# Five small reorderings at the seams of a two-block transformer kernel on one core

## The reference

```
def stick_breaking_attention(q, k, v):          # block 1, 8 heads of 64
    z = einsum('bhqd,bhkd->bhqk', qb, kb) * scale
    log_keep = where(mask, log_sigmoid(-z), 0.0)             # -softplus(z)
    suffix = cumsum(log_keep, reverse=True) - log_keep
    weights = where(mask, exp(log_sigmoid(z) + suffix), 0.0)
    ...
rv = proj columns for the values of retention   # block 1, "ret_v"
...
s = where(valid, (q_lat . c_sel + q_rope . r_sel) * scale, -inf)   # block 2, 8 sparse heads
p = softmax(s, axis=-1)                         # and 8 dilated heads after them
...
sc = einsum('bshd,bmhd->bhsm', qc, kvc[:, :, 0]) * CROSS_HEAD_DIM ** -0.5   # 4 heads of 256
pc = softmax(sc, axis=-1)
oc = einsum('bhsm,bmhd->bshd', pc, kvc[:, :, 1])
x = x + oc @ w_o_cross
x = x + square(relu(rmsnorm(x, norm_mlp_g) @ w_up)) @ w_down
return rmsnorm(x, norm_final_g)
```

## Time and profile before

| what | value |
|---|---|
| time, median of 3 runs (lowest, highest) | 1667.63 us (1666.0, 1667.67) |
| the profiled execution: time, span | 1664.19 us, 1662.4 us |
| PE busy | 1621.7 us, 98% of the span |
| weight loads of PE | 1318.5 us, 79% |
| DVE, ACT, POOL busy | 924.4 us (56%), 733.0 us (44%), 605.3 us (36%) |
| one split of a chunk on POOL (L148, mean of 91), on ACT (L142) | 4.61 us, 1.91 us |
| mean granted TensorE clock | 0.995 of full speed |

### The profile page before, as it was taken

One profiled execution on the slowest core, in us unless ns is written; L12 is line 12 of the kernel. 1 busy time (PEld: TensorE's weight loads), 2 busy tenths in 40 slices (PEclk: granted clock), 3 DMA queues, 4 the chain that ended last, 5 costly groups with the idle time before them and its releaser, 6 DMA issues.

```text
span 1662.4 us, 21089 instructions
## 1 busy us (share of the span) xinstructions
PE 1621.7 (98%) x7972; PEld 1318.5 (79%) x7972; DVE 924.4 (56%) x1116; ACT 733.0 (44%) x880; POOL 605.3 (36%) x253
## 2 busy tenths in 40 slices
PE   9999999999999999999999999999999999999996
PEld 7988888588887888888898668667877888888885
DVE  6244210682465799898967689893433552232313
ACT  5345222334344788878853332674333322221221
POOL 1412264134342243222313645663422444344441
PEclk9999999999999999999999999999999999999998
DMA  5211153212235999999954314101321222222221
GB/s 195 102 52 51 38 152 114 79 73 101 101 107 178 396 421 406 390 392 395 376 228 146 101 63 154 67 1 48 132 74 51 79 98 101 101 101 89 95 95 51
DMA packets 47139, 249.25 MB, mean 150 GB/s; under 512 B 9472, under 2 KB 10240, under 8 KB 20704
## 3 DMA queue, kind: packets, MB, share of 16 engines
q1 hardware_dynamic: 40880, 235.75, 38.2%
q0 software_dynamic: 5184, 8.40, 1.3%
q10 hardware_dynamic: 1008, 4.19, 0.6%
HBM read 236.05 MB, written 16.78 MB: 152 GB/s over the span
## 4 chain that ended last, share of the span: by engine, by line
PE 77%; issue 11%; DVE 6%; POOL 3%; ACT 2%; DMA 1%; SPq 0%; POOLq 0%; DVEq 0%; ACTq 0%
PE psum L229 22%; PE psum L231 21%; PE psum L230 21%; POOL w_lo L148 3%; PE psum L2208 2%; DVE kept_bias L2075 1%; DVE top L2074 1%; PE psum L662 1%; PE psum L2243 1%; PE psum L2231 1%; PE psum L1244 1%; PE psum L2479 1%; PE psum L681 1%; DMA raw<-in_w_dense 1%; PE psum L2499 1%
## 5 line engine op out<-in xcount | busy, mean ns | idle before, releaser
L148 POOL TENSOR_TENSOR w_lo<-raw,w_hi 128x2048 fp32r<-128x2048 f32 x91 | 419.2, 4606 | 701.6 <-ACT w_hi L142 663.3
L142 ACT ACTIVATE w_hi<-raw 128x2048 fp32r<-128x2048 f32 x96 | 183.4, 1910 | 313.8 <-PE psum L231 313.8
L229 PE MATMUL psum<-x_hi,w_hi 128*128 128x512 f32 x808 | 316.5, 392 | 1.4 <-POOL w_lo L148 0.7
L230 PE MATMUL psum<-x_lo,w_hi 128*128 128x512 f32 x808 | 314.4, 389 | 0.0
L231 PE MATMUL psum<-x_hi,w_lo 128*128 128x512 f32 x808 | 314.4, 389 | 0.0
L1262 DVE TENSOR_TENSOR moe_lo<-moe_w,moe_hi 128x2048 fp32r<-128x2048 f32 x100 | 227.7, 2290 | 31.0 <-ACT moe_hi L1252 29.9
L1252 ACT ACTIVATE moe_hi<-moe_w 128x2048 fp32r<-128x2048 f32 x100 | 190.9, 1915 | 30.1 <-PE psum L231 17.8
L229 PEld LDWEIGHTS psum<-x_hi,w_hi 128*128 128x128 f32 x808 | 151.7, 188 | 35.0 <-issue 2.0
L230 PEld LDWEIGHTS psum<-x_lo,w_hi 128*128 128x128 f32 x808 | 151.7, 188 | 31.7 <-issue 0.7
L231 PEld LDWEIGHTS psum<-x_hi,w_lo 128*128 128x128 f32 x808 | 151.7, 188 | 31.7
L434 DVE TENSOR_TENSOR res<-res,psum 128x512 f32<-128x512 f32 x56 | 38.4, 687 | 214.4 <-PE psum L231 214.4
(11 more groups left out here) (377 smaller groups left out, 2914.7 us busy)
## 6 DMA issues: line engine op xcount, KB each, us to landing
raw<-in_w_dense SPq DMA_DIRECT2D x96, 1024.0 KB, 4.8
moe_w<-in_w_moe_ahead SPq DMA_DIRECT2D x54, 1024.0 KB, 14.3
moe_w<-in_w_moe SPq DMA_DIRECT2D x48, 1024.0 KB
yrow<-expert_rows SPq DMA_DIRECT2D x8, 512.0 KB, 7.9
res<-in_x SPq DMA_DIRECT2D x4, 512.0 KB, 6.4
decay<-in_decay SPq DMA_DIRECT2D x8, 256.0 KB, 5.0
hn_rows<-hn_tok ACTq DMA_DIRECT2D x4, 512.0 KB, 7.8
out<-res SPq DMA_DIRECT2D x4, 512.0 KB, 2.7
```

The lines of the kernel that those rows point to most:

```text
L142: act.activation(w_hi[c % RING][:, :], raw[c % RING][:, :], ACT.Copy).then_inc(hi_ready, 1)
L148: pool.tensor_tensor(w_lo[c % RING][:, :], raw[c % RING][:, :], w_hi[c % RING][:, :].bitcast(F32), ALU.subtract).then_inc(lo_ready, 1)
L229: pe.matmul(out, lh, rh, start=first, stop=False)
L230: pe.matmul(out, lh, rl, start=False, stop=False)
```

## The change

Nothing that is computed changes. What moves:

1. In stick-breaking DVE makes `softplus(0)` before `size(1)` and `logs_low(0)` before it reads out tile 2.
2. The second tile of a head that has two (tiles 4, 6, 8, 10 and 13: `SECOND_V`) goes to bank 6 and not to bank 7. Bank 6 also holds the values of a pair of heads, so such a tile waits for `y_low` of the pair before from head 2 on, and `values` waits until bank 6 is read out.
3. ACT loads the exp table behind the sixth tile of v_b, takes the first exp of head 0 (`weigh(act, 0, 0)`) behind the seventh, and splits the second chunk of out2 (`split_hi`) only behind the exps of head 1. POOL's `split_lo` of that chunk moves behind all of its normalising in attention. DVE normalises head 0 before the softmax of head 1. dil_bias is loaded ahead of the chunks that v_b loads.
4. In cross attention the last head is turned into banks 4 and 5, which are spent once exp(2) is done, so that `transposes(2)` and `transposes(3)` stand before `values(2)` and `values(3)`. On DVE `normalise(3)` stands before the roundings of head 1.
5. The last norm sums squares by token: matmuls with one output column give 128x4 sums, root and reciprocal are taken of 128x4, DVE widens the result to 128x512 (`last_wide`), four transposes spread it in bank 5, and the eight scalings read it from PSUM. The square of the last tile is not added by DVE; it is a second group of four matmuls into the same columns.

```
@@ sticks_tensor, sticks_vector
+    SECOND_V = [tiles_of(h)[1] for h in range(HEADS) if TILES_V[h] == 2]
-            if j >= 1:
-                pe.wait_ge(bank_free, V_T + j + 4)
+            if j in SECOND_V:
+                pe.wait_ge(bank_free, V_T + j + 3)
+            elif j >= 1:
+                pe.wait_ge(bank_free, V_T + j + 4 - (j - 1 in SECOND_V))
...
+            pe.wait_ge(bank_free, V_T + 4 + max(j + 1 for j in SECOND_V if j < UPTO_V[min(2 * p + 1, HEADS - 1)]))
...
+                if j in SECOND_V and h >= 2:
+                    pe.wait_ge(y_low, h // 2)
                 ret_v_tile(j)
...
+        softplus(0)
         size(1)
-        softplus(0)
+        logs_low(0)
         ret_v_out(2)
-        logs_low(0)
@@ project_sync, project_gpsimd, project_scalar
+                if name == "v_b":
+                    sp.wait_ge(x1_done, KT)
+                    sp.wait_ge(tables_done, 4)
+                    sp.wait_ge(bank_free, FIRST_TILE["q_rope"] + 4)
+                    sp.dma_start(dil_bias[:, :], d["dil_bias"]).then_inc(a_in, 16)
...
-        dense_pool(pool, "v_b")
+        dense_pool(pool, "v_b", splits=1)
...
-            scale=tok_r12[:, j % 4:j % 4 + 1]).then_inc(bank_free, 1))
+            scale=tok_r12[:, j % 4:j % 4 + 1]).then_inc(bank_free, 1), splits=1,
+            tile_hooks={5: lambda: act.preload_act_table_set("exp_and_others"), 6: lambda: weigh(act, 0, 0)})
@@ attend_vector, attend_scalar, attend_gpsimd
+        softmax(0, 0)
+        softmax(0, 1)
         normalise(0)
+        softmax(1, 0)
+        softmax(1, 1)
...
-        exp(1, 0)
-        exp(1, 1)
+        weigh(act, 1, 0)
+        weigh(act, 1, 1)
+        split_hi(act, FIRST_CHUNK["out2"] + 1, FIRST_TILE["out2"])
...
             ins.then_inc(s_norm_pool, 1)
+        split_lo(pool, FIRST_CHUNK["out2"] + 1)
@@ cross_stage_tensor
-            if h >= 1:
+            if h == CH_HEADS - 1:
+                pe.wait_ge(cs_exp, COUNTED + CH_HEADS - 1)
+            elif h >= 1:
                 pe.wait_ge(ct_read2, COUNTED + h)
...
-        for h in range(CH_HEADS):
+        for h in range(CH_HEADS - 2):
             transposes(h)
-            if h + 2 < CH_HEADS:
-                scores(h + 2)
+            scores(h + 2)
+            values(h)
+        for h in range(CH_HEADS - 2, CH_HEADS):
+            transposes(h)
+        for h in range(CH_HEADS - 2, CH_HEADS):
             values(h)
@@ mlp_vector
+        dve.wait_ge(last_rooted, ONCE + 1)
+        link(dve, dve.reciprocal(last_rstd[:, :], last_rms[:, :]))
+        dve.tensor_copy(last_wide[:, :, :], wide(last_rstd[:, :], [P, TB, P], 2)).then_inc(last_turned, 1)
+        dve.wait_ge(last_spread, ONCE + 1)
+        for kt in range(KT):
...
+            dve.scalar_tensor_tensor(out=res[:, kt, :], in0=res[:, kt, :], scalar=norm_end2.gain_of(kt),
+                                     in1=psum[:, 5, :], op0=ALU.mult, op1=ALU.mult).then_inc(n_scaled, 1)
@@ mlp_tensor
-        norm_end2.pe(pe)
+        pe.wait_ge(n_added, (KT - 1) * norm_end2.u + KT - 2)
+        for q in range(TB):
+            pe.matmul(psum[:, 4, q:q + 1], norm_end2.sum[:, q * P:(q + 1) * P], ones[:, 0:1], start=(q == 0), stop=False,
+                      skip_group_check=True)
+        pe.wait_ge(n_squared, KT * (norm_end2.u + 1))
+        for q in range(TB):
+            mm = pe.matmul(psum[:, 4, q:q + 1], norm_end2.sq[1][:, q * P:(q + 1) * P], ones[:, 0:1], start=False, stop=True,
+                           skip_group_check=True)
+        mm.then_inc(last_summed, 1)
+        pe.wait_ge(last_turned, ONCE + 1)
+        for q in range(TB):
+            mm = pe.transpose(psum[:, 5, q * P:(q + 1) * P], last_wide[:, q, :], ident[:, :])
+        mm.then_inc(last_spread, 1)
```

More of the change, by code:

```diff
@@ L176, in dense_sync, with dense_pool @@
         loop(sp, n, body)
-    def dense_pool(pool, name, after=None, halves_first=False):
+    def dense_pool(pool, name, after=None, halves_first=False, splits=2):
         n, k = turns(name)
@@ L189, in dense_pool, with dense_act @@
         loop(pool, n, body)
-    def dense_act(act, name, evac=None, hooks=None, ahead=True):
+    def dense_act(act, name, evac=None, hooks=None, ahead=True, tile_hooks=None, splits=2):
         n, k = turns(name)
@@ L204, in body @@
                     evac(act, i, j, (t0 + j) % 4)
-                if ahead or i < n - 1:
+                    if tile_hooks and j in tile_hooks:
+                        tile_hooks[j]()
+                if b < splits and (ahead or i < n - 1):
                     split_hi(act, c0 + 2 + b, t0 + per * (b + 1), i, k * per * i)
@@ L2313, in attend_vector, with weigh @@
                 low((k - 3) // 2)
+    def weigh(act, h, part):
+        b = h % 3
+        scale = (HD + 32) ** -0.5 if h < HEADS else HD ** -0.5
+        act.wait_ge(s_read, COUNTED + 2 * h + part + 1)
+        for qt in ((3,), (2, 1, 0))[part]:
+            n = P * (qt + 1)
+            ins = act.activation(score_of(h)[:, SEG[n]:SEG[n] + n], score_of(h)[:, SEG[n]:SEG[n] + n], ACT.Exp,
+                                 bias=snmax[b][:, qt:qt + 1], scale=scale, accum_out=ssum[b][:, qt:qt + 1])
+        if part:
+            ins.then_inc(s_exp, 1)
     def attend_scalar(act):
@@ L2350, in attend_scalar @@
             if k + 2 < A_HEADS:
-                exp(k + 2, 0)
+                weigh(act, k + 2, 0)
             if k < A_HEADS:
@@ L2415, in high @@
             act.activation(y_hi[:, t, :], psum[:, 2 + t % 2, :], ACT.Copy).then_inc(cv_high, 1)
-        for h in range(CH_HEADS):
+        for h in range(CH_HEADS - 2):
             copy_t(h)
-            if h + 2 < CH_HEADS:
-                exp(h + 2)
+            exp(h + 2)
             high(2 * h)
             high(2 * h + 1)
+        for h in range(CH_HEADS - 2, CH_HEADS):
+            copy_t(h)
+        for t in range(2 * CH_HEADS - 4, 2 * CH_HEADS):
+            high(t)
         residual_act(act, "o_cross", norm_mlp, root=False, gained=lambda t: norm_mlp.high_gained(act, t))
@@ L2551, in mlp_scalar @@
             else:
-                residual_act(act, name, norm_end2)
+                residual_act(act, name, norm_end2, root=False)
+                act.wait_ge(last_summed, ONCE + 1)
+                act.activation(last_rms[:, :], psum[:, 4, 0:TB], ACT.Sqrt, scale=1.0 / D, bias=col("eps"))\
+                   .then_inc(last_rooted, 1)
     def mlp_vector(dve):
@@ L2604, in _ @@
             project_sync(sp)
-            attend_sync(sp)
             cross_stage_sync(sp)
```

58 lines of the change are left out of this document (29 added, 29 removed).

## The result

The changed kernel takes 1654.72 us (median of 5 runs, 1654.38 to 1660.36) against 1667.63 before: ratio 0.993, 95% interval 0.9916 to 0.9944. It is faster by 0.7%, or 11.7 us by the ratio and 12.9 by the medians. The forecast of 1656.9 was 2.2 us high; its gain of 10.7 us is less than either figure.

What follows compares the result with a forecast made beforehand. TensorE, busy 98% of the span, was taken to bound the kernel. Terms of -1.45, -3.75, 0, 0, -1.9 and -3.6 sum to -10.7 us, giving 1656.9 from the median 1667.63; range 1653.5 to 1661.5.

Steps and rivals of the forecast that it cites:

- first hole of stick-breaking: TensorE's 1.4 us wait before the first suffix sums goes as softplus(0) starts earlier on DVE: -1.45 us.
- bank 6, five places: Stick-breaking: five second value tiles no longer wait for the first one's copy, 0.75 us each: -3.75 us.
- attention's start: The wait at head 0 goes, but the same time is waited at heads 1 and 2: 0, bounds -2.2 and +0.9.
- POOL's split, dil_bias: Split after attention ends 8.6 us before out2 wants the chunk; dil_bias loads on an almost empty queue: cost 0.
- cross attention: Values of heads 2 and 3 run without a hole, one of about 0.7 stays: -1.9 us, bounds -2.3 and -1.0.
- tail: Last norm: 3.1 us from a shorter chain, square to first scaling, 0.5 from shorter scalings: -3.6, bounds -4.0 and -2.5.
- the holes only move: Rival in stick-breaking: bank 7's holes only move, the stage gives 1.4 instead of 5.2 us, total 1660.7; 8%.
- attention gains too: Rival at attention's start: ACT's split is hidden and both holes go, sum -12.9 us, total 1654.7; 12%.
- the half microsecond for a shorter step of the scalings: Tail: eight scalings with an operand in PSUM step in 0.60 instead of 0.67 us, 0.5 us gained.
- Slower by GpSimd: Rival at out2's second chunk: each microsecond POOL's split ends after 1141.9 is one of TensorE; 1671 us, 3%.
- the turning point: Delay of POOL's split from which the kernel is slower than before by 3.3 us: 22.6 us (8.6 + 10.7 + 3.3).

Runs made afterwards that it cites:

- the one run with a delay: The changed kernel with GpSimd's moved split of out2's second chunk done four times over, each waiting for the one before: 1664.10 us in one run.
- the second measurement: The same changed kernel run once more with nothing altered: 1654.39 us, ratio 0.9929 to the kernel before.

## Why the prediction was right

Each step of the forecast against what the traces give:

| step | forecast | measured |
|---|---|---|
| first hole of stick-breaking | -1.45 | -1.80 |
| bank 6, five places | -3.75 | -3.98 |
| attention's start | 0 (-2.2 to 0.9) | -0.16 |
| POOL's split, dil_bias | 0, cover 8.6 | 0, cover 8.7 |
| cross attention | -1.9 | -1.99 |
| tail | -3.6 | -3.26 |
| sum | -10.7 | -11.2 |

- **Stick-breaking.** Order and waits are as forecast, none of the new waits (`y_low`, bank 6) shows. Both terms were too small, by 0.35 and by 0.23, because the way back to pace was priced at 0.05 for the one hole and 0.19 for each of the others; it was 0.4 and 0.24. The rival that the holes only move is refuted by each edit run alone.
- **Attention.** The two holes that take the first one's place are where the forecast said, at head 1 and at the scores of head 4, and the price of the split decides between them and a gain: with it moved, 0.62 came. The rival "attention gains too" overrated its prize: with the split hidden the stage gave 0.8 in all and not 2.2, as DVE is next.
- **Cross attention.** One hole of 0.65 in front of transposes(3), forecast 0.7; the values of both heads without a gap. The roundings that values(3) wants, forecast 0.1 us ahead of need, end 0.20 ahead of its matmuls.
- **Tail.** The chain was right: 2.82 for 2.95 from the last square to the first scaling; the widening took 0.43, less than its estimate of 0.55. The mis-sized term is the half microsecond for a shorter step of the scalings. It was read off scalings that multiply by a number, and went to scalings that multiply by a column; the 0.06 us a step are the column's. The Trainium skill (VectorE: DVE Perf Modes, "The TRN2 errata") would have had the scalings with an operand in PSUM 0.065 slower each, an estimate from its 120 and 58 cycles; the trace has them at 0.66 with it and without. So neither the rule nor the forecast's use of its row holds here: moving the operand to PSUM changed nothing. And had the step come down, 0.2 of the 0.5 would have reached the end.
- **Slower by GpSimd.** The cover was right. The slope was not: "each microsecond is one of TensorE" leaves out the clock, and 5.2 us of waiting cost 7.5. For that reason the turning point lies nearer than 22.6 us of delay, by some 2 us if the one run with a delay is a guide (an estimate from it).

The mechanism of every stage was right but for the step of the scalings; of the errors in size the two largest partly cancel, since stick-breaking gave 0.6 more than forecast and the tail 0.3 less. That the measured 1654.72 is the very time of the rival "attention gains too" (1654.7) is chance: its gain of 2.2 at attention's start was 0.16 in the trace, and the time alone could not have told the two apart.

The medians differ by 12.9, the terms add up to 11.2. Between them lie the columns that belong to no edit. The interval of the ratio (-9.3 to -14.0 us) and that of the second measurement (0.9917 to 0.9942) hold 11.2; whether the remaining 0.5 us (by the ratio) to 1.7 (by the medians) is chance, or the shorter tail also suffers less from a lower clock (0.5 and 0.7 in two of its eight traces, 0.3 to 1.0 in three of six with the old one), is left open.

## What to carry to other kernels

Find what each wait in the list is worth by adding what TensorE needs to get back to its pace (0.2 to 0.4 us here), and when a hole is closed ask which engine is late next: here it was ACT, then DVE, and in the tail the transfers. A split that is moved off one wait must go into a gap of its engine, not behind the next thing that is waited for; the trace names the gap. Compare two traces by the distance between like instructions, stage by stage, before a loss is put down to an edit: three stretches here moved by 1.0 to 2.1 us between traces of kernels that don't differ there, beside a lower granted clock.

## What the runs showed of the hardware

- The same instructions get different clocks: of 14 traces, six had 1.5 us more at 1037:1087 than their edits account for, each with a granted clock of 0.58 to 0.88 in one or two windows of 4 us between 1020 and 1036; in the other eight it was 1.00 there. How much of the spread of single runs (1664.5 to 1669.0 in 27 of the kernel before) this and the like behind the router make is not shown, as these runs have no trace: the fastest of them had the highest mean clock, 0.997, but the 16 with a mean clock of 0.994 spread from 1665.0 to 1669.0.
- After 5.2 us without a matmul the granted clock was 0.50, and the next nine stepped in 0.43 instead of 0.23 us.
- A 128x512 multiply with three inputs on VectorE steps in 0.66 us with a column of scalars, whether its second tensor lies in SBUF or in PSUM, and in 0.60 with a number (one of its tensors in PSUM); a plain product with PSUM steps in 0.60.
- Products of 128x512 on VectorE (one tensor in SBUF, one in PSUM) and on GpSimd (both in SBUF) at the same time took 0.60 and 1.25 us each, no more than alone (1.29 for products of GpSimd in the kernel before).
- Writing from SBUF to HBM on one core, four queued transfers of 512 KB ran at 403 GB/s, eight of 256 KB at 380.
